# A hybrid attention, mLSTM and mixture-of-experts layer: separate semaphores for one third of attention's operand loads, and merge weights issued one unit earlier

## The reference

```python
h = rmsnorm(x, g_norm_mix); proj = h @ w_in            # split into 14 parts
y_att   = dsa_attention(aq, ak, av, iq, ik, iw)        # 8 heads of 64, 2 key/value heads
hm      = rmsnorm(mlstm_chunkwise(mq, mk, mv, i_pre, f_pre))
y_mlstm = sigmoid(mo) * hm
merged  = sigmoid(ga) * (y_att @ w_proj_att) + sigmoid(gm) * (y_mlstm @ w_proj_mlstm)
x = x + merged @ w_out
return x + hierarchical_moe(rmsnorm(x, g_norm_moe), ...)
```

## Time and profile before

| | us |
|---|---|
| median of 3 runs | 3233.22 |
| the three runs | 3233.22, 3232.07, 3250.53 |
| profiled execution, its time | 3236.73 |
| profiled execution, its span | 3235.0 |
| TensorE busy | 2932.3 (91%) |
| attention, first issue to last matmul | 1180.9 to 1855.5 |
| merge, first issue to last unit | 1861.6 to 2235 |
| mean granted TensorE clock | 0.964 |

### The profile page before, as it was taken

One profiled execution on the slowest core, in us unless ns is written; L12 is line 12 of the kernel. 1 busy time (PEld: TensorE's weight loads), 2 busy tenths in 40 slices (PEclk: granted clock), 3 DMA queues, 4 the chain that ended last, 5 costly groups with the idle time before them and its releaser, 6 DMA issues. The chain is left out here.

```text
span 3235.0 us, 46841 instructions
## 1 busy us (share of the span) xinstructions
PE 2932.3 (91%) x13280; PEld 2268.0 (70%) x13280; DVE 2556.0 (79%) x3842; ACT 1989.1 (61%) x2852; POOL 951.4 (29%) x977
## 2 busy tenths in 40 slices
PE   7998899899899967889889979999499999999997
PEld 5765678778678844555556558888378877888886
DVE  6577589899999969789887564444589989999997
ACT  5322367678578726667667743333277777878775
POOL 0211100000000033444333200000046676666664
PEclk9999999999999978899999989999799999999999
DMA  3222422222212255565443464564278988968895
GB/s 130 85 74 75 118 78 78 67 72 75 73 59 68 69 123 121 145 134 104 113 94 58 97 217 150 182 183 127 101 248 261 362 284 306 356 215 287 265 322 162
DMA packets 354858, 496.35 MB, mean 153 GB/s; under 512 B 32464, under 2 KB 197632, under 8 KB 354576
## 3 DMA queue, kind: packets, MB, share of 16 engines
q1 hardware_dynamic: 327680, 409.42, 41.1%
q0 software_dynamic: 25440, 84.26, 9.5%
q10 hardware_dynamic: 1584, 0.79, 0.1%
HBM read 485.64 MB, written 113.58 MB: 185 GB/s over the span
## 5 line engine op out<-in xcount | busy, mean ns | idle before, releaser
L981 DVE TENSOR_TENSOR e_w_lo<-e_raw,e_w_hi 128x1024 fp32r<-128x1024 f32 x386 | 447.2, 1216 | 8.2 <-ACT e_w_hi L832 7.6
L1640 PE MATMUL x_ps<-h_hi,w_hi 128*128 128x512 f32 (+1 forms) x992 | 390.7, 394 | 5.6 <-PEq L90 4.5
L832 ACT CAST e_w_hi<-e_raw 128x1024 fp32r<-128x1024 f32 x386 | 378.7, 1052 | 20.3 <-DMA e_raw<-in_w_exp_up 13.3
L1640 PE MATMUL x_ps<-h_lo,w_hi 128*128 128x512 f32 (+1 forms) x992 | 389.0, 392 | 0.0
L1640 PE MATMUL x_ps<-h_hi,w_lo 128*128 128x512 f32 (+1 forms) x992 | 388.3, 391 | 0.0
L1827 DVE TENSOR_SCALAR_CACHE_REDUCE x_relu<-x_score,x_cand 128x1024 uint8<-128x1024 f32 (+3 forms) x217 | 315.7, 1487 | 3.6
L1742 ACT ACTIVATE x_relu<-x_score,x_cand 128x896 int8<-128x896 f32 (+3 forms) x217 | 281.0, 1297 | 59.5 <-DVE x_cand L1834 59.3
L2538 DVE CUSTOM_DVE_ANT_0 t_junk<-t_L,shared 128x512 bf16<-128x512 f32 (+3 forms) x320 | 186.1, 604 | 80.6 <-PE t_L L2288 78.8
L768 PE MATMUL e_pG<-e_w_hi,e_x_hi 128*128 128x512 f32 x768 | 242.6, 397 | 5.5 <-DVE e_x_lo L976 5.5
L2508 ACT ACTIVATE t_probT<-t_ST 128x512 f32<-128x512 f32 x272 | 161.4, 593 | 133.0 <-PE t_ST L2317 121.9
L768 PE MATMUL e_pG<-e_w_lo,e_x_hi 128*128 128x512 f32 x768 | 238.5, 392 | 0.0
(11 more groups left out here) (432 smaller groups left out, 7369.6 us busy)
## 6 DMA issues: line engine op xcount, KB each, us to landing
e_raw<-in_w_exp_gate SPq DMA_DIRECT2D x392, 256.0 KB
e_raw<-in_w_exp_up SPq DMA_DIRECT2D x392, 256.0 KB
shared<-in_w_exp_down SPq DMA_DIRECT2D x192, 512.0 KB
projT<-x_out SPq DMA_DIRECT2D x120, 256.0 KB, 2.3
w_raw<-in_w_in SPq DMA_DIRECT2D x40, 512.0 KB, 4.6
o_gate<-projT SPq DMA_DIRECT2D x32, 512.0 KB
a_tables<-in_x SPq DMA_DIRECT2D x16, 512.0 KB, 5.4
qkT<-shared SPq DMA_DIRECT2D x32, 256.0 KB, 3.5
```

What stands on the lines that cost most here:

```text
L832: nc.scalar.copy(w_hi[:, u, :], raw[:, u, :]).then_inc(gh, 1)
L981: nc.vector.tensor_tensor(w_lo[:, u, :], raw[:, u, :], w_hi[:, u, :].bitcast(F32), ALU.subtract).then_inc(gl, 1)
L1640: last = nc.tensor.matmul(ps[0:w, u % 4, :], wt[:, m % 2, kk, 0:w], ht[:, kk, q * 512:(q + 1) * 512], start=(kk == 0 and s == 0), stop=(kk ...
```

## The change

Attention: the third transfer of each block of queries, and of each 512 columns of keys, adds to a semaphore of its own (`q2_in`, `k2_in`). `logits` waits for 32, so for the two transfers that it reads, and `logits_t` waits for the third ahead of its third matmul, at the first key block of a step with v = 0 (queries) and at the first use of each 512 columns (keys). The order and number of transfers stay.

Merge: SP issues `weights(u + 3)` where it issued `weights(u + 2)`, and `weights(2)` ahead of `SUM`. What each waits for stays.

```diff
--- before.py
+++ after.py
@@ -233,12 +233,14 @@
             gates(0)
             weights(1)
             gates(1)
+            weights(2)
             sp.dma_start(SUM[:, :], last(pg.d["exp_sums"])).then_inc(sum_in, 16)
             for g in range(NGRP):
                 for m in range(KT):
                     u = g * KT + m
+                    if u + 3 <= LASTM:
+                        weights(u + 3)
                     if u + 2 <= LASTM:
-                        weights(u + 2)
                         gates(u + 2)
                     if u == 2:
                         sp.dma_start(G[:, :], i["g_norm_moe"].partition_broadcast(P)).then_inc(consts, 16)
@@ -1966,7 +1968,8 @@
         setup, idf_ok, idb_ok, row_ok = (sem(n) for n in ("setup", "idf_ok", "idb_ok", "row_ok"))
         k_in = [sem(f"k_in{q}") for q in range(NKC)]
         v_in = [sem(f"v_in{q}") for q in range(NKC)]
-        q_in = [sem(f"q_in{b}") for b in range(4)]
+        q_in, q2_in = ([sem(f"{z}_in{b}") for b in range(4)] for z in ("q", "q_high"))
+        k2_in = [sem(f"k_high_in{q}") for q in range(NKC)]
         mk_in = [sem(f"mask_in{b}") for b in range(4)]
         y_st = [sem(f"y_stored{b}") for b in range(2)]
         mk_set, l_ok, mx_ok, nm_ok, d_ok, st_ok, p_ok, ph_ok, pl_ok, pv_ok, ou_ok, vh_ok, vl_ok = (sem(n) for n in (
@@ -2000,7 +2003,7 @@
                 src = queries(n)
                 for k in range(2):
                     sp.dma_start(Q[k * AD:(k + 1) * AD, n % 4, :, :].bitcast(F32), src[0]).then_inc(q_in[n % 4], 16)
-                sp.dma_start(Q2[0:AD, n % 4, :, :].bitcast(F32), src[1]).then_inc(q_in[n % 4], 16)
+                sp.dma_start(Q2[0:AD, n % 4, :, :].bitcast(F32), src[1]).then_inc(q2_in[n % 4], 16)
                 if n >= 2:
                     sp.dma_start(MB[:, n % 4, 0:width(n)], pg.d["mask"][n][:, 0:width(n)]).then_inc(mk_in[n % 4], 16)
 
@@ -2044,7 +2047,7 @@
                 keys = pg.d["k_parts"].rearrange("s (v d) n -> s d v n", d=AD)[:, :, :, part]
                 for k in range(2):
                     sp.dma_start(KS[k * AD:(k + 1) * AD, :, part].bitcast(F32), keys[k]).then_inc(k_in[q], 16)
-                sp.dma_start(K2[0:AD, :, part].bitcast(F32), keys[0]).then_inc(k_in[q], 16)
+                sp.dma_start(K2[0:AD, :, part].bitcast(F32), keys[0]).then_inc(k2_in[q], 16)
 
             def load_values(q):
                 if q:
@@ -2280,9 +2283,9 @@
                 n, v = STEPS[s]
                 h, (lo, hi) = v * R4 + x // len(parts(n)), parts(n)[x % len(parts(n))]
                 if x == 0 and v == 0:
-                    pe.wait_ge(q_in[n % 4], 48 * (n // 4 + 1))
+                    pe.wait_ge(q_in[n % 4], 32 * (n // 4 + 1))
                 if n == lo // P and v == 0:
-                    pe.wait_ge(k_in[lo // 512], 48)
+                    pe.wait_ge(k_in[lo // 512], 32)
                 if made >= 3:
                     pe.wait_ge(mx_ok, made - 2)
                 nc.tensor.matmul(L[:, made % 3, 0:hi - lo], Q[:, n % 4, h, :], KS[:, v, lo:hi], start=True, stop=True).then_inc(l_ok, 1)
@@ -2314,6 +2317,10 @@
                 keys = slice(j * P, (j + 1) * P)
                 nc.tensor.matmul(o, KS[:, v, keys], Q[:, n % 4, v * R4:(v + 1) * R4, :], start=True, stop=False)
                 nc.tensor.matmul(o, MB[:, n % 4, keys], idb[:, :].unsqueeze(1).broadcast_to([P, R4, P]), start=False, stop=False)
+                if v == 0 and j == 0:
+                    pe.wait_ge(q2_in[n % 4], 16 * (n // 4 + 1))
+                if v == 0 and n == j and j % 4 == 0:
+                    pe.wait_ge(k2_in[j // 4], 16)
                 nc.tensor.matmul(o, K2[0:AD + 1, v, keys], Q2[0:AD + 1, n % 4, v * R4:(v + 1) * R4, :], start=False, stop=True).then_inc(st_ok, 1)
 
             def values(s, j):
@@ -2477,7 +2484,7 @@
                     a.activation(SQ[:, :, :], N1[:, :, 0:MD], ACT.Square).then_inc(sq_ok, 1)
             for k in range(2):
                 act.dma_start(Q[k * AD:(k + 1) * AD, 0, :, :].bitcast(F32), queries(0)[0]).then_inc(q_in[0], 16)
-            act.dma_start(Q2[0:AD, 0, :, :].bitcast(F32), queries(0)[1]).then_inc(q_in[0], 16)
+            act.dma_start(Q2[0:AD, 0, :, :].bitcast(F32), queries(0)[1]).then_inc(q2_in[0], 16)
 
             def values_high(q):
                 act.wait_ge(v_in[q], 16)
```

## The result

| | before | after |
|---|---|---|
| median of 15 runs, us | 3229.33 | 3211.93 |
| lowest and highest, us | 3225.78 to 3254.57 | 3203.99 to 3233.39 |
| profiled execution, its span, us | 3235.0 | 3231.7 |
| merge, first transfer to last product, us | 425.5 | 410.2 |
| attention, first issue to last matmul, us | 673.2 | 673.9 |

A forecast was written before the change was run, and what follows sets the result against it. Group 0 of the merge was taken as bound by when weights land, then by the gates' loop. Attention's 2.6 us and the merge's 7.4 made 10.0 us less, 3223 us for the median from 3233.2, range 3214 to 3231.

The forecast's parts named there:

- (b): Merge, group 0: weights of unit u + 3 leave earlier, so the 13.0 us of stalls vanish apart from the first 1.6.
- Weights that come earlier can give nothing there: Merge, groups 1 to 3 and the products: PE busy 296.4 of 300.4 us, so earlier weights gain 0.
- 37.2 + 4.1: Merge, sum 1 to sum 7: three loops of the gates, 37.2 us, plus bursts of 2.5 and 1.6 us.
- The bursts: Merge, group 0: transfers ahead of gates delay sum 7, residual blocks by 2.5 us and constants by 1.6 us.
- first rival: Merge, group 0: matmuls bind, units take 5.6 us each, gain 15.4 us, 3215 in all with attention; chance 0.17.
- (a): Merge, group 0: SUM behind unit 2's weights delays unit 1 by 1.4 us, bounds 0 and 2.7.
- Where gates bind, PE has room for that, so I count nothing: Merge, group 0: half-clock stretches after PE stalls, 1.7 us of matmul each, were put at 0.
- The lower bound: Attention's start: only PE's own path counts, as block 1's query wait ends earlier, gaining 1.4 us.
- if attention ends where it did: Attention's end: a stated sign that the forecast is wrong, against the 2.6 us gain taken for the stage.
- second rival: Attention: its gain is swallowed by later short waits, leaving only the merge's 7.4 us, 3226; chance 0.17.
- The products wait for sum 7: Merge, end of group 0: the products start after sum 7, so its earlier arrival gains the stage 7.4 us.
- slower rival: Merge, group 0: gates land behind full sets of weights, 10.5 us a landing, kernel 2.5 us slower, 3236; chance 0.06.

The follow-up runs named there:

- early_g0: The changed kernel with weights early only for units 2 to 7 of group 0, old order from unit 8 on: 3221.04 us, 0.9960 of before.
- early_g13: The changed kernel, attention's part included, with weights early only from unit 9 on (groups 1 to 3): 3222.30 us, 0.9959 of before.
- merge_only: Only the merge's part of the change, attention as before: 3213.83 us, 0.9930 of before.
- q1_first: The changed kernel with block 1's first two query transfers issued ahead of the keys' third and the values: 3213.75 us, 0.9944 of before.
- res_late: The changed kernel with the two residual blocks issued behind the gates of unit 7 instead of unit 6: 3218.58 us, 0.9949 of before.
- sum_first: The changed kernel with SUM issued ahead of weights(2) again: 3209.47 us, 0.9916 of before.
- late3: Before's attention, early weights and three further merge edits, with PE also waiting for block 1's queries ahead of its first matmul: 3211.76 us, 0.9950 of before.
- late8: Before's attention, early weights and three further merge edits, with PE also waiting for block 2's queries ahead of its first matmul: 3214.28 us, 0.9941 of before.
- all_split: The change plus SUM ahead of weights(2), residual blocks behind unit 7's gates, router-weights wait at the first router matmul: 3211.31 us, 0.9946 of before.

## Why the prediction was wrong

The mechanism of (b) was right, the sum was not. That the time fell outside the range is in part the base (3.9 us, above); but the step of point 1 is wrong by the traces, whatever the base. Point by point:

1. **"Weights that come earlier can give nothing there" is the step that failed.** It was read from 296.4 us busy of 300.4, and put at 0; it is 6.1 us from the first product to the last (353.4 to 347.3 us), shown by early_g0 and early_g13. Even as a bound the 4.0 idle us were too few, as stalls between pipelined matmuls hide in busy time. In before the eight units of a group took 45.0, 44.9 and 45.3 us, in after 43.64 each time, and 192 spacings of 0.227 us are 43.6: 4.3 us. The other 1.8 us are in the products between them.
2. **Merge, group 0: 7.4 us forecast, 9.3 measured** at sum 7 in after (69.7 to 60.4), and 13.2 in merge_only and 8.6 in q1_first, whose merges are the same. The 6.3 us of a gate's landing held. The way from sum 1 to sum 7 took 36.6 us, not 37.2 + 4.1: sums 2 and 3 followed PE's units, and only from unit 4 on did the gates hold them. Then two units took 11.5 and 12.2 us (sums 4 to 6 and 5 to 7), near the forecast's 12.4. The bursts were priced as if each stood in the path (2.5 us for the residual blocks, about 0.9 in res_late), and PE was taken to follow the gates, while its two output buffers let it run on. Units 2 to 7 ran as the first rival said (chance 0.17), 5.6 us apart on average. That rival's 15.4 us did not come, since sum 7 was held by its gates and the half clock fell on unit 1.
3. **(a) held at unit 1**, 1.4 us forecast, 1.5 measured (12.4 to 13.9), 1.7 back in sum_first. Its follow-up was missed: the longer idle time was followed by 6.8 us at 0.50, so that unit 2 came 4.2 us later. "Where gates bind, PE has room for that, so I count nothing" was too cheap. Fewer stalls did bring less half clock: from the first transfer to the last matmul of unit 7 it is 20.0 us in before and 13.0 in after, 16.5 to 20.0 in the four profiles with the old order of weights in group 0, and 6.1 to 13.1 in the twelve with early weights. The rule cited in the forecast from the Trainium skill (TensorE: Matmul & The Clock Gate, Part 1), that half rate is the default and activity releases it, agrees with that.
4. **Attention: 2.6 us taken, 1.2 measured** at `shift_row(0)`, as a mean of eight profiles with the split in the old order (19.1) against four without (20.3). First logits 4.2 earlier, 4.5 forecast. The lower bound, PE's own path with 1.4 us, was the right row; GpSimd's path also ended only 1.5 us earlier, because its second half waited 2.63 us for maxima of logits that had moved by 0.4 us in that execution. But nothing of it is seen at the end: the stage took 673.2 us before and 673.9 after, and 674.0 on average in the four profiles without the split, 675.6 in the eight with it, under a spread of 7 us that goes with the clock. By the forecast's own sign, wrong "if attention ends where it did", this part fails. Its second rival, that the gain is swallowed (chance 0.17), is not ruled out, though late3 and late8 speak against slack. The third matmul's waits cost nothing that shows.
5. "The products wait for sum 7" was the wrong releaser with the right time: the router weights follow sum 7 by a fixed chain, 2.4 to 2.5 us from the start of the one to the first product in before and after, so the number was unharmed. But 3.9 to 8.6 us of PE stood idle there in the nine profiles with that wait, which no rival named, and before's row for it, 3.86 us behind `o_router`, was there to be read.
6. The slower rival (gates behind weights) did not occur: landings of 5.7 to 7.4 us. They are far from 2 us, in a stage that moved 256 GB/s up to its first product. The figure cited in the forecast, about 2 us of fixed cost, stands in the Trainium skill (DMA: Bandwidth & Descriptors, Anatomy of one DMA) for a transfer issued by GpSimd, beside a part that grows with size; alone it does not give these landings of SP's transfers.

The sum with the measured terms is 9.3 + 6.1 = 15.4 us, which is the stage's 15.3, and 16.6 if attention's 1.2 us reach the end; the medians differ by 17.4, with 12 to 24 as interval, so the total can't tell the two apart.

## What to carry to other kernels

A stretch in which an engine is 98.7% busy can still hold 2% of time. Compare the spacing of its instructions with the smallest spacing they ever show, and count the units' pace, before a prefetch there is put at nothing. Where an engine waits ahead of a stage, read which wait is written there, not which one is logical: moving a wait from ahead of the products to its first user brought the first product 3.6 to 4.4 us forward in before and 3.3 to 8.8 with early weights. And a gain at the head of a stage should be followed to the second wait, for it was there that 3.8 of attention's 4.2 us went.

## What was not expected of the hardware

- Recorded matmuls of 0.39 us start every 0.227 us. A stall shows 0.16 us shorter as idle time than it is, and the next spacing is 0.1 us longer (in before a spacing of 0.87 us, then one of 0.33).
- With the same instructions, the second half of attention took 363.4 to 363.5 or 366.4 to 367.8 us, with two or with three to five stretches at clock 0.50. Over the whole stage 82.5 to 99.5 us were at half clock. What decides between them stays open; PE's work was the same.
- The half clock at unit 1 goes with PE's idle time ahead of it, though not strictly. With 1.4 to 1.6 us of idle time (nine profiles, sum_first's 1.37 among them) no stretch at 0.50 stands there. With 1.93 (all_split), 2.67, 2.74 and 3.03 us (early_g0) it is 3.4 us long, and with 2.89 (q1_first), 2.99 and 3.05 us (after) 6.8 us.
